# Modulation weights as the moving operand, the first norm's squares on ScalarE, the first head's k product moved up: a change to the front of a three-block transformer kernel on one Trainium2 core

## The reference

```python
cond = jax.nn.silu(c); cond_ctx = jax.nn.silu(c_ctx)
mod   = cond @ w_mod[l] + b_mod[l]          # (1024) @ (1024, 6144)
mod_c = cond_ctx @ w_mod[l] + b_mod[l]
sh1, sc1, gt1, sh2, sc2, gt2 = split(mod, 6)   # and csh1, csc1 of mod_c
hx = rms_norm(x, norm1_g) * (1 + sc1) + sh1    # x:   512 x 1024
hc = rms_norm(ctx, norm1_g) * (1 + csc1) + csh1  # ctx: 256 x 1024
# delta_prep: p = h @ w_in
k, v = silu(conv(p[..., :2048])); ba = p[..., 2048:2080]   # 32 columns
beta = sigmoid(ba[:2]); g = -exp(a_log) * softplus(ba[2:] + dt_bias)
```

## Time and profile before

| | us |
|---|---|
| median of three runs | 3245.92 |
| lowest, highest | 3240.98, 3254.99 |
| the profiled execution | 3252.46 |
| its span, first to last instruction | 3250.8 |
| TensorE (PE) busy in it | 3088.6 (95%), 17542 records |
| VectorE, ScalarE, GpSimd busy | 1065.9, 745.5, 223.6 |
| share of the chain that ended last | PE 91%, DVE 4%, ACT 3%, issue 2% |

### The profile page before, as it was taken

The page is one execution under the profiler, slowest core; times in us unless marked ns, Lnnn a source line. Parts: engine busy times, 40 slices in busy tenths (PEclk is TensorE's granted clock), DMA queues, the critical chain, the costliest instruction groups (busy, mean ns, idle before and its releaser), DMA issues.

```text
span 3250.8 us, 42898 instructions
## 1 busy us (share of the span) xinstructions
PE 3088.6 (95%) x17542; PEld 1818.8 (56%) x17542; DVE 1065.9 (33%) x2052; ACT 745.5 (23%) x1427; POOL 223.6 (7%) x273
## 2 busy tenths in 40 slices
PE   7799999999999999999998998999999999999998
PEld 6577777777444443444444556665555545575443
DVE  2355555555222224444212115541101322352100
ACT  0333333333300002111003115540000031363000
POOL 0011221222000000000001001000000010100000
PEclk9999999999989999999998999999999999999999
DMA  5000000000324433444222110001111121101222
GB/s 179 20 21 28 28 28 21 28 28 21 136 97 136 135 110 103 155 155 154 92 86 68 43 41 30 2 14 45 52 52 45 52 68 52 43 1 40 73 76 71
DMA packets 59737, 213.56 MB, mean 66 GB/s; under 512 B 6337, under 2 KB 8769, under 8 KB 59330
## 3 DMA queue, kind: packets, MB, share of 16 engines
q1 hardware_dynamic: 42512, 153.11, 14.7%
q0 software_dynamic: 12800, 49.29, 4.4%
q10 hardware_dynamic: 4274, 8.95, 0.8%
HBM read 209.23 MB, written 2.10 MB: 65 GB/s over the span
## 4 chain that ended last, share of the span: by engine, by line
PE 91%; DVE 4%; ACT 3%; issue 2%; POOL 0%; ACTq 0%; DMA 0%; DVEq 0%
PE psum L323 88%; PE psum L675 3%; DVE arena L1267 1%; DVE arena L1250 0%; DVE arena L1247 0%; POOL arena L1671 0%; DVE arena L1255 0%; ACT arena L855 0%; ACT arena L904 0%; DVE arena L1531 0%; ACTq L861 0%; DMA arena<-in_ctx2T 0%; PE psum L510 0%; ACT arena L1110 0%; DVE psum L1523 0%
## 5 line engine op out<-in xcount | busy, mean ns | idle before, releaser
L323 PE MATMUL psum<-arena 64*64 64x64 f32 (+9 forms) x16614 | 2980.7, 362 | 152.4 <-ACT arena L855 24.2
L323 PEld LDWEIGHTS psum<-arena 128*128 128x128 f32 (+4 forms) x16614 | 1719.4, 166 | 1393.4 <-issue 1186.8
L1377 DVE SCALAR_TENSOR_TENSOR arena<-arena 128x1024 f32<-128x1024 f32 x128 | 149.2, 1221 | 3.9 <-DMA arena<-in_mods 3.9
L1624 DVE SCALAR_TENSOR_TENSOR arena<-arena,psum 128x512 f32<-128x512 f32 x32 | 21.2, 685 | 381.3 <-PE psum L323 381.3
L1065 ACT ACTIVATE arena<-psum,arena 128x768 f32<-128x768 f32 (+1 forms) x160 | 129.1, 813 | 53.3 <-DVE arena L1513 19.4
L675 PE MATMUL psum<-arena 128*128 128x128 f32 x832 | 109.6, 278 | 1.1 <-ACT arena L1065 1.0
L1124 ACT ACTIVATE arena<-psum 128x512 f32<-128x512 f32 x32 | 19.1, 598 | 382.1 <-PE psum L323 382.1
L675 PEld LDWEIGHTS psum<-arena 128*128 128x128 f32 x832 | 89.9, 140 | 28.5 <-issue 24.4
L1691 POOL DMA_DIRECT2D arena<-in_bias x16 | 8.8, 554 | 1218.8 <-DVE arena L1496 826.8
L1054 ACT ACTIVATE arena<-psum 128x512 f32<-128x512 f32 x128 | 69.9, 595 | 97.5 <-PE psum L675 97.5
L1685 POOL DMA_DIRECT2D arena<-in_mods x76 | 40.3, 530 | 693.2 <-DVE arena L1377 693.2
(11 more groups left out here) (187 smaller groups left out, 1359.9 us busy)
## 6 DMA issues: line engine op xcount, KB each, us to landing
arena<-in_stream SPq DMA_DIRECT2D x288, 512.0 KB, 3.6
arena<-in_mods POOLq DMA_DIRECT2D x80, 512.0 KB, 3.6
arena<-in_bias POOLq DMA_DIRECT2D x16, 448.0 KB, 4.2
arena<-in_xT ACTq DMA_DIRECT2D x1, 2048.0 KB, 13.2
out<-arena SPq DMA_DIRECT2D x1, 2048.0 KB, 7.2
arena<-in_conds ACTq DMA_DIRECT2D x1, 1536.0 KB
arena<-in_ctxT ACTq DMA_DIRECT2D x1, 1024.0 KB, 15.5
arena<-in_lnrows ACTq DMA_DIRECT2D x1, 1024.0 KB
```

Of the source, the lines that this page charges most:

```text
L323: return pe.matmul(out, lhsT, rhs, start=start, stop=stop, skip_group_check=True)
L1377: m = stt(mjunk[:, b % 2, :] if x < len(conds) - 1 else slot, slot, 0.5, cb[:, c, :], ALU.mult, ALU.mult, accum_out=dst(x))
```

## The change

The modulation weights are packed by rows instead of by blocks: a tile holds 128 rows (one slice k) and 1024 columns (half hf). They are now the moving operand, 512 columns at a time, and the conditions are the stationary one: `condp`, 128 x 32 for each slice, of which columns 0 and 1 are filled and the rest are zero. The results lie in rows, in one bank, with j and hf choosing the partitions 0, 32, 64 or 96 (the column group). After the last tile VectorE copies the bank to `pre_rows`, and four small matmuls with columns of `ident` turn the rows into columns, to which VectorE adds the bias.

The squares of the first norm are made by ScalarE, as soon as x and ctx are there, into two alternating slices, and TensorE adds each with `ones` (`norm_step`), one after each of the tiles 6 to 13. VectorE makes none.

For beta and the gates `wba` is stationary (128 x 32) and `H` moves; each slice of `H` is taken as soon as it is finished, slice k into column group k mod 4. The four groups are copied out by ScalarE (x) and VectorE (ctx) and added up, and turned, by six matmuls with `sum4`. Step 0 of the first head's k product stands before that, steps 1 to 7 behind it, ahead of the cumulative sums. The product was behind the transposes before.

The DMAs of ident, wba and con1 go to GpSimd's queue, ahead of its memsets. From 16 on the tiles of the stream are unchanged.

```diff
@@ scalar
-            act.dma_start(wba, a_wba).then_inc(s("small"), 16)
-            act.dma_start(ident, a_ident).then_inc(s("small"), 16)
-            act.dma_start(con1, a_con1).then_inc(s("small"), 16)
             act.wait_ge(s("vecs"), 16)
-            f(flat(gt[:, 2])[:, 0:32], vec("cond", 0, 32), ACT.Tanh, scale=0.5).then_inc(s("condt"), 1)
-            act.wait_ge(s("small"), 16 * 3)
+            f(flat(gt[:, 2])[:, 0:16], vec("cond", 0, 16), ACT.Tanh, scale=0.5).then_inc(s("condt"), 1)
+            act.wait_ge(s("x_in"), 32)
+            norm_squares(0)
             norm_root(0, (1, 2), True)
             norm_shift(0, ((0, SEQ, 0), (SEQ, TOK, 1)), modT[:, 0:8, :])
-
-            act.wait_ge(s("ba"), 1)
+            act.wait_ge(s("front"), 2)
+            f(ba_rows[:, 0:SEQ], psum[:, 5, :], ACT.Copy).then_inc(s("front_rows"), 1)
+
+            act.wait_ge(s("front"), 3)
@@ tensor
-            with pe.Fori(0, 4) as i:
-                pe.wait_ge(s("pre_mod"), i + FREE)
-                mods(T_PRE, 4, 0, 0, i, 4)
-            norm_sums(0, (1, 2), True)
+            for t in range(16):
+                k, hf = divmod(t, 2)
+                w = weights(pe, T_PRE + t)
+                for j in range(2):
+                    r = 32 * (2 * hf + j)
+                    m = mm(psum[r:r + 32, 0, :], condp[:, k, :], w[:, SEQ * j:SEQ * (j + 1)], k == 0, k == KT - 1)
+                m.then_inc(s("used"), 1)
+                if 6 <= t < 6 + KT:
+                    norm_step(0, t - 6, (1, 2))
             pe.wait_ge(s("small"), 16 * 3)
-
-
-            pe.wait_ge(s("H"), KT)
+            pe.wait_ge(s("front_rows"), 1)
+            for q in range(4):
+                m = mm(psum[:, 4, 8 * q:8 * q + 8], pre_rows[:, q * P:(q + 1) * P],
+                       ident.rearrange("p (j c) -> p j c", j=4)[:, :, 0:2])
+            m.then_inc(s("front"), 1)
+            for k in range(KT):
+                pe.wait_ge(s("H"), k + 1)
+                r = 32 * (k % 4)
+                mm(psum[r:r + 32, 5, :], wba[:, k, :], H[:, k, 0:SEQ], k < 4, k >= 4)
+                m = mm(psum[r:r + 32, 6, 0:CTX], wba[:, k, :], H[:, k, SEQ:TOK], k < 4, k >= 4)
+            m.then_inc(s("front"), 1)
+            steps(T_HEAD, range(0, 1), 0, 1, 0)
+            pe.wait_ge(s("front_rows"), 3)
             for c in range(CH):
-                for k in range(KT):
-                    m = mm(psum[:, 3, 32 * c:32 * c + 32], H[:, k, coff(c):coff(c) + P], wba[:, k, :],
-                           k == 0, k == KT - 1)
-            m.then_inc(s("ba"), 1)
+                m = mm(psum[:, 3, 32 * c:32 * c + 32], ba_rows[:, c * P:(c + 1) * P], sum4)
+            m.then_inc(s("front"), 1)
+            steps(T_HEAD, range(1, KT), 0, 1, 0)
             pe.wait_ge(s("g"), 1)
@@ tensor, ahead of the head loop
-            steps(T_HEAD, range(KT), 0, 1, 0)
@@ tensor, the new helper
+            def norm_step(n, k, banks):
+                pe.wait_ge(s("nsq"), KT * SQUARED[n] + k + 1)
+                mm(psum[:, banks[0], 0:SEQ], ones, sqb[:, k % 2, 0:SEQ], k == 0, k == KT - 1)
+                m = mm(psum[:, banks[1], 0:CTX], ones, sqb[:, k % 2, SEQ:TOK], k == 0, k == KT - 1)
+                m.then_inc(s("nsum" if k == KT - 1 else "sq_read"), 1)
@@ vector
+            dve.memset(condp, 0.0).then_inc(s("ones"), 1)
...
-            squares_begin(0)
-            with dve.Fori(0, 4) as i:
-                dve.wait_ge(s("used"), 4 * i + 4)
-                tt(modT[:, bass.ds(4 * i, 4), :], psum[:, 0, 0:8].rearrange("p (a b) -> p a b", a=4),
-                   vecs[:, bass.ds(VEC["b_mod"] + 4 * i, 4), None].to_broadcast([P, 4, 2]), ALU.add)\
-                    .then_inc(s("pre_mod"), 1)
-                dve.wait_ge(s("x_in"), 32)
-                for j in range(2):
-                    squares_add(0, 2 * i + j, TOK)
+            dve.wait_ge(s("used"), 16)
+            dve.tensor_copy(pre_rows, psum[:, 0, :]).then_inc(s("front_rows"), 1)
+            dve.wait_ge(s("front"), 1)
+            tt(modT[:, 0:16, :].rearrange("p (j q) c -> p j q c", q=4),
...
+            dve.wait_ge(s("front"), 2)
+            dve.tensor_copy(ba_rows[:, SEQ:TOK], psum[:, 6, 0:CTX]).then_inc(s("front_rows"), 1)
@@ gpsimd
+            pool.dma_start(ident, a_ident).then_inc(s("small"), 16)
+            pool.dma_start(wba, a_wba).then_inc(s("small"), 16)
+            pool.dma_start(con1, a_con1).then_inc(s("small"), 16)
             pool.memset(gcT[0:64, :], 0.0).then_inc(s("Tz"), 1)
```

More of the change, by code:

```diff
@@ L35 @@
 START = {"G": 2, "u": 4, "xo": 4, "xd": 4, "b2_z": 4, "b2_xo": 8}
-STREAMED = {0: 0, 1: 1, 2: 2, 4: 3}
+STREAMED = {1: 0, 2: 1, 4: 2}
+SQUARED = {0: 0, 3: 1}
 T_PRE = 0
@@ L69 @@
 _n = 0
-for _name, _w in (("level", LEVELS * 2 * HP), ("id64", HP), ("tri", 2 * P), ("sel", 16)):
+for _name, _w in (("level", LEVELS * 2 * HP), ("id64", HP), ("tri", 2 * P), ("sel", 16), ("sum4", 32)):
     CON1[_name] = _n
@@ L121, in build @@
         H = keep.take(KT, TOK)
-        condv = keep.take(2, KT, 2)
         modT = keep.take(48, 2)
@@ L167, in build @@
         wba = flat2(A)[:, 0:KT * 32].rearrange("p (k n) -> p k n", k=KT)
+        condp = flat2(eR)[:, 0:KT * 32].rearrange("p (k n) -> p k n", k=KT)
+        pre_rows = flat2(ktok)[:, 0:SEQ]
+        ba_rows = flat2(vtok)
         gt = arena[:, M_at:M_at + 12 * CH * 16].rearrange("p (a c n) -> p a c n", a=12, c=CH)
@@ L222, in build @@
         id64 = con1[:, CON1["id64"]:CON1["id64"] + HP]
+        sum4 = con1[:, CON1["sum4"]:CON1["sum4"] + 32]
         tri = con1[:, CON1["tri"]:CON1["tri"] + 2 * P].rearrange("p (d c) -> p d c", d=2)
@@ L337, in product @@
                 m.then_inc(s("used"), 1)
-            def mods(t, n, bank, which, i=None, per=0, j0=0):
-                for j in range(n):
-                    w = weights(pe, t + j, i, per)
-                    for k in range(KT):
-                        m = mm(psum[:, bank, 2 * (j0 + j):2 * (j0 + j) + 2], w[:, k * P:(k + 1) * P], condv[:, which, k, :],
-                               k == 0, k == KT - 1)
-                    m.then_inc(s("used"), 1)
             def norm_sums(n, banks, wide):
@@ L358, in norm_sums @@
                 for k in range(KT):
[L359 to L367, removed]
-            with pe.Fori(0, 4) as i:
-                pe.wait_ge(s("pre_mod"), i + FREE)
-                mods(T_PRE, 4, 0, 0, i, 4)
-            norm_sums(0, (1, 2), True)
-            pe.wait_ge(s("small"), 16 * 3)
-            pe.wait_ge(s("H"), KT)
-            for c in range(CH):
-                for k in range(KT):
-                    m = mm(psum[:, 3, 32 * c:32 * c + 32], H[:, k, coff(c):coff(c) + P], wba[:, k, :],
-                           k == 0, k == KT - 1)
-            m.then_inc(s("ba"), 1)
[L381 to L394, removed]
+                    norm_step(n, k, banks)
+            def norm_step(n, k, banks):
[3 more added lines that the diff above has]
+                m.then_inc(s("nsum" if k == KT - 1 else "sq_read"), 1)
             def steps(t, ks, bank, ctx_bank, i):
@@ L404, in steps @@
                     m.then_inc(s("used"), 1)
+            pe.wait_ge(s("ones"), 2)
+            pe.wait_ge(s("cond"), 2)
+            for t in range(16):
[7 more added lines that the diff above has]
+                    norm_step(0, t - 6, (1, 2))
+            pe.wait_ge(s("small"), 16 * 3)
+            pe.wait_ge(s("front_rows"), 1)
[11 more added lines that the diff above has]
+            pe.wait_ge(s("front_rows"), 3)
+            for c in range(CH):
+                m = mm(psum[:, 3, 32 * c:32 * c + 32], ba_rows[:, c * P:(c + 1) * P], sum4)
+            m.then_inc(s("front"), 1)
+            steps(T_HEAD, range(1, KT), 0, 1, 0)
+            pe.wait_ge(s("g"), 1)
+            for d in range(2):
+                mm(psum[:, 4, 48 * d:48 * d + 48], tri[:, d, :], gt[:, 0, :, 8 * d:8 * d + 8])
+            mm(psum[:, 4, 96:192], ones, flat(gt[:, 0])).then_inc(s("gcum"), 1)
+            pe.wait_ge(s("gc"), 2)
+            for c in range(CH):
+                for r in (0, 32):
+                    m = mm(psum[r:r + 16, 5 + c // 4, (c % 4) * P:(c % 4 + 1) * P], gt[:, 1, c, :], ident)
+            m.then_inc(s("gcum"), 1)
+            pe.wait_ge(s("gates"), 1)
+            pe.wait_ge(s("Tz"), 5)
             def next_k(n, i):
@@ L884, in _ @@
             f(gt[:, 10], gt[:, 11], ACT.Exp).then_inc(s("gex"), 1)
-            act.wait_ge(s("gcT"), 1)
+            act.wait_ge(s("gcum"), 2)
             act.wait_ge(s("Tz"), 5)
@@ L1090, in _ @@
                 if l == 0:
-                    norm_squares()
+                    norm_squares(3)
                 norm_root(3 + l, (0, 1), True)
@@ L1742, in pack_stream @@
     ga, gb = (wblocks(w_in[:, o + 4096 + 1024 * j:o + 5120 + 1024 * j]) for j in range(2))
-    mod = wblocks(a["w_mod"][0][:, 0:2048])
+    mod = a["w_mod"][0][:, 0:2048].reshape(KT, P, 2, D).transpose(0, 2, 1, 3).reshape(2 * KT, P, D)
```

(3 more changed lines are left out.)

17 lines of the change are left out of this document (11 added, 6 removed).

## The result

| | before | changed |
|---|---|---|
| median of the runs, us | 3243.45 (4 runs, 3240.38 to 3254.99) | 3201.32 (4 runs, 3194.57 to 3208.05) |
| ratio | | 0.9864 (95%: 0.9829 to 0.9898) |
| profiled execution, its span | 3252.46, 3250.8 | 3204.75, 3203.1 |

Timed a second time beside other kernels, the changed kernel's ratio was 0.9856 (0.9838 to 0.9875). The change takes off 42 us in the first medians and 48 in the second. The forecast was 3194 in a range of 3178 to 3216.

A forecast was written before the change was run, and what follows sets the result against it. TensorE, busy 95% of the span, was taken as the bound. The front's decay rows move from 133.65 to 81.3, saving 52.3 us: profiled 3200.2, median 6.5 below, so 3194; own range 3186 to 3202, with scatter 3178 to 3216.

The forecast's parts named there:

- first matmul: Start of the modulations: three small loads leave ScalarE's queue, so TensorE begins at 7.2 us instead of 14.58.
- ctx in: Landing of ctx beside the weight stream: 24 us taken, between bounds 17.7 and 28.7.
- step 0 of the norm: TensorE's first sum of squares, behind ScalarE's first square (0.84 us) once ctx is in: at 25 us.
- tile 15 through: End of modulations and norm sums: 25 + 17.9 + 3.2 for changes of form + 2.5 for low clock = 48.6 us.
- H starts: After the rows are turned into columns, 2.8 us new on the path: H starts at 51.4 us, before at 81.19.
- gates' products end: Beta and gates' products keep pace with H, 1.28 us per k, ending 1.9 after its last slice: 63.0 us.
- decay rows: First matmul of the head loop: at 81.3 us instead of 133.65, with 2.6 us idle before it.
- rival C: Modulations and gates' products: the column groups don't overlap; 3203 to 3209 us; chance 0.08.
- the hole at 19 us: TensorE stands still about 5 us awaiting ctx's first square; its clock falls, 5 us slow, 2.5 lost.
- Rival A: The clock stays low in the front: decay rows at 104, 30 us saved, 3216 us; chance 0.14.
- B: Data early: ctx in by 19, TensorE doesn't stop, 5 to 7.5 us more saved, 3187 us; chance 0.16.
- D: Slower than before: no overlap, so no high clock, rows drained 16 times; decay rows at 145, 3257 us; chance 0.03.

The follow-up runs named there:

- x_first: The changed kernel with X and ctx issued by SyncE ahead of the stream's first four tiles instead of by ScalarE beside them; ratio 0.9832, median 3190.1 us.
- cover_dummy: The changed kernel with three more 128 x 512 products, read by nothing, into an unused bank behind the transposes; ratio 0.9862, median 3203.2 us.

## Why the prediction was right, and where it wasn't

| step of the prediction | forecast us | measured us |
|---|---|---|
| first matmul | 7.2 | 6.15 |
| tiles 0 to 6 through | 19 | 20.8 |
| ctx in | 24 (17.7 to 28.7) | 28.57 |
| step 0 of the norm | 25 | 29.49 |
| tile 15 through | 48.6 | 52.3 |
| H starts | 51.4 | 54.64 |
| gates' products end | 63.0 | 65.8 |
| decay rows | 81.3 | 83.42 |
| first head, against before | 0 | 4.8 lost |
| time, against the median before | 52 less | 42 less, 48 in the second timing |

**The start** was a microsecond too long: the table load runs from 3.59 to 4.87, while vecs is still on its way (it landed at 5.4), so it is off the path.

**The late ctx** was the mis-sized term. I took 24 out of 17.7 to 28.7 on the ground that the ring fills up and leaves the DMAs to ctx. It does, but only after the tiles: the eleventh landed at 27.0, ctx at 28.6. The whole stretch has a DMA share of 0.99 at 378 GB/s, and the upper bound, all bytes that can come first over the rate, was met within 0.2 us. The bound would have been the better estimate. `x_first` shows the cause.

**The clock in the front** went as said in its order: up during the first tiles (1.69 us for a tile at 13.65, 1.05 at 15.69, the last records of a block overhanging), down in the hole, 0.56 on average from 29.49 to 36.30, and 1.00 from there to 56. I had 5 us slow where there were 6. Then it fell a second time, while the rows were turned, and the first 5.8 us of the gates' products ran at the low level:

```profile
57.00:62.80 5.80, 5.80 (x19) 2.67 (x21) 5.80 (x12) 5.80 (x11) 0.00 (x0) 0.50 0.02 4
```

The prediction took these products as fast (1.28 us a slice). It cost nothing, because ScalarE's slices of `H` set the pace here: its last one ended at 64.35 and TensorE 1.5 us later, at 65.8, where 1.9 was forecast.

**Column groups overlap**, so rival C falls. From 36.30 to 51.14 six tiles and six steps take 14.84 us, 2.47 a pair of them. A step alone is 1.28 and a tile in pairs 0.85; serial tiles would give 2.99 without any price for the changes of form. What is left, 0.34, I put down to the changes of form: 0.17 for each of two (0.2 forecast). The Trainium skill ("TensorEngine Tiling (Array Packing)", Key Properties) says that changing the mode drains the engine. The trace agrees in that each change costs time, with these 0.17 us. The products for the gates overlap too: 32 records in 8.82 us at a granted clock of 0.67, where one after another would need 10.2 at full clock, and more at 0.67.

**From H to the decay rows** the sum said 29.9 and it took 28.8. The gate arithmetic is hidden beside the k product, as forecast, and the copies of gcT stand open before the decay rows with 2.64 us, forecast as 2.6.

**What I left out** is what that pause costs beyond itself. I named the cover that goes and priced the 2.6 us, but not the clock behind it:

```profile
83.42:94.00 10.58, 10.52 (x16) 4.37 (x17) 6.32 (x17) 4.62 (x8) 1.29 (x2) 0.52 0.01 2
```

This is the 4.8 us that the first head is longer than before. The prediction reasoned just so for the hole at 19 us, and I didn't apply it to the pause before the decay rows. This term stood at nothing in the sum, and `cover_dummy` shows it. With it and the 2.1 us of the front the forecast for the profiled pair would have been 45, and 47.7 came; the difference is the 2.3 us of the rest, where no instruction was changed, and which I had no ground to expect.

**Rival A** (clock low in the whole front) fell with the 1.00 from 36 to 56 us; **B** was never near; **D** needed both C and A.

## What to carry to other kernels

When a change takes away what covers a pause of TensorE, price the pause twice: its own length, and the low clock behind it. The second price is due only where TensorE sets the pace: it was 4.8 us behind the pause before the decay rows, and nothing in the gates' products, which wait for ScalarE. If there is nothing useful to move there, even matmuls that nobody reads kept the clock up in that place, though here the whole kernel was no faster for them. Where a load is awaited by everything, issue it ahead of a stream that can refill itself: beside such a stream, the estimate for when it lands is the sum of all bytes that can come first over the rate (28.7 against 28.6 measured). And a gain of 10 us in the front of a kernel of 3200 need not show in its time: the later falls of the clock differ in number and length from kernel to kernel, so compare stretches with the same instructions before the total is believed.

## What the runs showed of the hardware that I had not expected

The same 202 matmul records between two fixed points took 79.1, 80.7 or 83.9 us, with a granted clock of 0.87, 0.85 and 0.82, in three kernels that differ only in their front; over the whole rest the kernels' spread was 11.7 us, 0.4% of the time. The same pause of 2.6 us before the decay rows was followed by 34.6 us for the first head in the changed kernel and 31.4 in `x_first`.

A DMA issued ahead of the others on its queue isn't alone on the engines: in `x_first` ctx, issued 1.6 us after the start, behind x and ahead of the whole stream, took 13.2 us to land, where I had expected 9. By 14.84 us 4.56 MB had been moved: x and ctx (3.15), vecs, ident, wba and con1 on the other queues (0.97), and 0.44 of the stream.
